# Two token groups in turn: the first 128 prompt tokens go through the trunk of a hybrid decoder step alone, and their expert rows are fetched while the other 136 tokens go through it

## The reference, cut to what matters

```python
def layer(x):                                  # x: 256 prompt rows, then 8 sample rows
    z, xbc, dt, q, k, v, iq, ik, iw, g_a, g_b = split(rms_norm(x, norm1_g) @ w_in)   # 1024 -> 10368
    y_ssd = ssd(conv(xbc), dt, z)              # prompt: 2 chunks of 128, state handed on; sample: one step
    y_att = sparse_attention(q, k, v, iq, ik, iw)   # prompt: best 64 keys; sample: best 256 of a paged cache
    merged = sigmoid(g_a) * (y_ssd @ w_branch_a) + sigmoid(g_b) * (y_att @ w_branch_b)
    x = x + merged @ w_out
    return x + peer(rms_norm(x, norm2_g))

def peer(h, p):
    q = (h @ p['peer_wq']).reshape(n, 8, 2, 128)
    s = einsum('nhcd,chkd->nhck', q, p['peer_keys'])        # 2 x 128 scores a head
    s1, i1 = top_k(s[:, :, 0], 16);  s2, i2 = top_k(s[:, :, 1], 16)
    top_s, pos = top_k(s1[..., :, None] + s2[..., None, :], 16)   # of 256 sums
    g = softmax(top_s)
    act = gelu(einsum('nd,nhkd->nhk', h, p['peer_u'][eidx]))
    return einsum('nhk,nhkd->nd', g * act, p['peer_v'][eidx])
```

## Time and profile before

| | before |
|---|---|
| median of 3 runs | 1549.29 us (1548.42 to 1551.8) |
| the profiled execution | 1551.73 us, its span 1550.1 us |
| mean granted TensorE clock | 0.944 |
| PE, DVE, ACT, POOL busy | 82%, 56%, 39%, 28% of the span |
| moved by the DMA engines | 391.08 MB, mean 252 GB/s |
| span up to the first expert gather | 859.65 us |

### The profile page before, as it was taken

One profiled execution on the slowest core, in us unless ns is written; L12 is line 12 of the kernel. 1 busy time (PEld: TensorE's weight loads), 2 busy tenths in 40 slices (PEclk: granted clock), 3 DMA queues, 4 the chain that ended last, 5 costly groups with the idle time before them and its releaser, 6 DMA issues. The chain is left out here.

```text
span 1550.1 us, 18152 instructions
## 1 busy us (share of the span) xinstructions
PE 1265.0 (82%) x4972; PEld 768.5 (50%) x4972; DVE 864.0 (56%) x2312; ACT 608.0 (39%) x1556; POOL 432.5 (28%) x510
## 2 busy tenths in 40 slices
PE   5968999999677877699989678977976787878777
PEld 4846678777555555488878323322322322222222
DVE  1025459998192427650110798898995554544544
ACT  1125237878382414500001345443533444444443
POOL 1331002220121200000000354644787333333331
PEclk8978999999697988999999799999999999999999
DMA  4543223322387630144142799999996999999997
GB/s 157 171 156 99 80 82 122 110 96 93 129 311 288 207 106 1 67 173 169 55 158 87 313 421 400 421 421 409 397 421 284 419 422 423 421 422 422 422 422 317
DMA packets 77066, 391.08 MB, mean 252 GB/s; under 512 B 11384, under 2 KB 22168, under 8 KB 39616
## 3 DMA queue, kind: packets, MB, share of 16 engines
q0 software_dynamic: 43168, 287.34, 45.4%
q1 hardware_dynamic: 33088, 101.32, 18.8%
q10 hardware_dynamic: 736, 1.56, 0.3%
HBM read 378.43 MB, written 11.60 MB: 252 GB/s over the span
## 5 line engine op out<-in xcount | busy, mean ns | idle before, releaser
L1706 PE MATMUL pe_acc<-pe_uv,pe_dg 128*128 128x512 f32 (+1 forms) x1056 | 524.8, 624 | 147.5 <-ACT pe_dg L1752 143.9
L1932 DVE CUSTOM_DVE_ANT_0 pe_uv<-pe_uv,pe_hnat 128x1024 f32<-128x1024 f32 x264 | 321.4, 1219 | 195.5 <-DMA pe_uv<-d_uv,pe_idx 183.9
L1706 PEld LDWEIGHTS pe_acc<-pe_uv,pe_dg 128*128 128x128 f32 (+1 forms) x1056 | 180.1, 189 | 488.8 <-ACT pe_dg L1752 342.3
L1799 POOL DMA_INDIRECT pe_uv<-d_uv,pe_idx x256 | 319.1, 1246 | 337.4 <-PE pe_acc L1706 314.1
L180 PE MATMUL pi_ps<-xn,pi_w 128*128 128x264 f32 x944 | 226.6, 397 | 9.5 <-PEq L86 9.5
L180 PEld LDWEIGHTS pi_ps<-xn,pi_w 128*128 128x128 f32 x944 | 182.4, 197 | 42.2 <-issue 11.3
L1746 ACT ACTIVATE pe_gl<-pe_a 128x1 f32<-128x1 f32 x264 | 53.4, 202 | 351.4 <-DVE pe_a L1932 348.6
L1752 ACT ACTIVATE pe_dg<-cst,pe_w 128x128 f32<-128x128 f32 x256 | 102.8, 401 | 8.3
L1749 ACT ACTIVATE pe_w<-pe_gl,pe_gw 128x1 f32<-128x1 f32 x256 | 75.4, 295 | 31.5
L1781 POOL COPY pe_hrep<-hN 128x128 f32<-128x128 f32 x8 | 1.9, 295 | 298.0 <-POOLq L86 298.0
L1613 PE MATMUL pq_ps<-hN,pq_w 128*128 128x264 f32 x256 | 58.7, 393 | 5.7 <-DMA pq_w<-d_wq 5.7
(11 more groups left out here) (283 smaller groups left out, 1707.8 us busy)
## 6 DMA issues: line engine op xcount, KB each, us to landing
pi_w<-d_w_in SPq DMA_DIRECT2D x71, 512.0 KB, 3.3
mg_w<-d_w_ab SPq DMA_DIRECT2D x8, 1536.0 KB, 6.7
ss_h<-d_state SPq DMA_DIRECT2D x8, 1024.0 KB, 7.1
o_ssm_s<-ss_h SPq DMA_DIRECT2D x8, 1024.0 KB, 7.1
pq_w<-d_wq SPq DMA_DIRECT2D x16, 512.0 KB, 3.3
lg_w<-d_w_in SPq DMA_DIRECT2D x10, 512.0 KB, 6.1
paged<-d_ck POOLq DMA_DIRECT2D x32, 128.0 KB, 5.5
paged<-d_ck SPq DMA_DIRECT2D x32, 128.0 KB, 5.5
```

The source lines that it names most:

```text
L1706: mm = pe.matmul(acc[0:m, 4 * half:4 * half + 4, :], lhsT, uv[:, r, D_MODEL + half * 512:D_MODEL + (half + 1) * 512], start=False, stop=Fa ...
L1799: pool.indirect_dma_start(uv[:, r, :], None, k.d_uv[:], bass.IndirectOffsetOnAxis(ap=src, axis=0)).then_inc(gathered[r], 16)
L1932: dve.tensor_tensor_reduce(uv[:, r, 0:D_MODEL], uv[:, r, 0:D_MODEL], hnat[:, n, :], 1.0, 0.0, ALU.mult, ALU.add, a[:, r:r + 1]).then_inc(d ...
```

## The change

Token group 0 is the first 128 prompt tokens, group 1 the other 128 prompt tokens and the 8 samples (136 columns). The 81 projection tiles are still computed once, for all 264 tokens, and their results are written to two sets of buffers. From there the blocks run twice, in this order: `attend_prompt(0)` (16 slots; all 32 rounds of the sample's top-256 and 44 tiles), `time_steps` (now 6 tiles), `ssd_chunk(0)`, `merge(0)`, `queries(0)`; then `attend_prompt(1)`, `attend_sample`, `ssd_chunk(1)`, `merge(1)`, `queries(1)`. `merge` and `queries` load all of their weights in both turns. `LastGates` is gone.

The experts are a class now. Units go in pairs; a pair is three pieces of code, which the blocks of group 1 put behind their own work of slot m on DVE, of slot m+1 on ACT and of slot m+2 on PE. Group 0's 64 pairs are dealt out over five blocks; the other 68 run at the end of `queries(1)`. The ring has 6 slots. A unit's product is four matmuls of 64 rows and 64 columns of the array in place of two of 128 by 128; for it ACT makes two 128x64 folded diagonals. In the diff `END` is all 81 tiles, `j` is `p % 8` (a head has 8 pairs), and `attend` runs all up to `merge(0)`. K and V pages come on SP's queue alone.

```diff
-    ends = [Z0, Z0 + 6, Z0 + 14, END - BANKS, END]
+    ends = [Z0, Z0 + 6, Z0 + 14, END - 6, END]
...
+    ends = [0, 12, 36, 43, 54, 64]
+    pairs = [list(range(a, b)) for a, b in zip(ends, ends[1:])]
...
+            attend(nc, k, prompt)
+            ex = Experts(nc, last, k)
+            queries(nc, k, ex, 0, [])
+            k.hankel[1], = tensors(nc, prompt, hankel1=(P, HEADS, TP))
+            attend_prompt(nc, k, 1, [], ex, pairs[0])
+        attend_sample(nc, k, ex, pairs[1])
+    k.Y[1], k.rms[1] = tensors(nc, trunk, Y1=(P, KI, W), rms1=(P, GROUPS, W))
+    ssd_chunk(nc, k, 1, ex, pairs[2])
+    merge(nc, k, 1, ex, pairs[3])
...
+            queries(nc, k, ex, 1, pairs[4])
...
+def late(at, m, lag):
+    return at[m - lag] if 0 <= m - lag < len(at) else []
...
+class Experts:
+    RING, PAIRS = 6, 4
+    def gathers(self, pool, pairs):
+        end = min(2 * pairs[-1] + 2 + self.RING, self.UNITS) if pairs else self.RING
+        for u in range(self.sent, end):
+            n, i = self.tile(u)
+            if n < 2 and i % TOPK == 0:
+                pool.wait_ge(self.indexed, self.choice(u) + 1)
+            if n == 2 and i == 0:
+                pool.wait_ge(self.moved, 64)
+            if u >= self.RING:
+                pool.wait_ge(self.accumulated, u - self.RING + 1)
+            pool.indirect_dma_start(self.uv[:, u % self.RING, :], None, self.k.d_uv[:], ...)
+        self.sent = end
+    def dots(self, dve, p):
+        for u in (2 * p, 2 * p + 1):
+            dve.wait_ge(self.gathered[r], 16 * (u // self.RING + 1))
+            dve.tensor_tensor_reduce(self.uv[:, r, 0:D_MODEL], self.uv[:, r, 0:D_MODEL], h[:], ...)
+        if j == 0:
+            self.choosing = self.choose(dve, follows)    # the next head's choice, in 21 pieces
+        if j < 4:
+            for _ in range(7):
+                next(self.choosing, None)
+        elif j == 6:
+            self.weights(dve, follows)
+    def weigh(self, act, p):
+        act.wait_ge(self.dotted, 2 * p + 2)
+        act.activation(self.gl[:, q, :], self.a[:, q, :], ACT.Gelu_apprx_tanh).then_inc(self.gelued, 1)
+...
+    def mix(self, pe, p):
+        for u in (2 * p, 2 * p + 1):
+            pe.wait_ge(self.diagonal, u + 1)
+            for half in range(2):
+                for q in range(2):
+                    rows = slice(q * HD, (q + 1) * HD)
+                    mm = pe.matmul(self.acc[half * HD:(half + 1) * HD, q, :], self.dg[rows, r, :],
+                                   self.uv[rows, r, vals], start=False, stop=False, ...)
+            mm.then_inc(self.accumulated, 1)
...
 def ssd_chunk, DVE's list, for g in range(GROUPS):
                 dve.wait_ge(em_ready, g + 1)
                 dve.tensor_tensor(mx[:, g % 2], em[:, g % 2], cb[:, g, :]..., ALU.mult).then_inc(mixed, 1)
+                for p in late(at, g, 0):
+                    ex.dots(dve, p)
...
 def merge, PE's list, for n in range(KD):
-                branch(n, pa, range(KI), lambda c: k.Y[:, c, :]).then_inc(multiplied, 1)
+                branch(n, pa, range(KI), lambda c: Y[:, c, :]).then_inc(multiplied, 1)
+                for p in late(at, n, 2):
+                    ex.mix(pe, p)
...
 def attend_sample, POOL's list:
-            for visit in range(2 * VK):
-                load(pool, by_pool, 1, visit)
+            ex.gathers(pool, todo)
```

More of the change, by code:

```diff
@@ L51 @@
 GATE0 = XBC0 + N_XBC
[L52 to L53 removed]
+END = N_TILES
 Q0, K0, V0, IQ0 = 0, 8, 10, 12
@@ L661, in _, with attend_prompt @@
             dve.wait_ge(read, 1)
-def attend_prompt(nc, k, tiles):
+def attend_prompt(nc, k, part, tiles, ex=None, pairs=()):
     NL, NPR, LAG_T, LAG_O = 3, 4, 2, 3
@@ L908, in _, with ssd_chunk @@
             mm.then_inc(widened, 1)
-def ssd_chunk(nc, k, c):
-    t0 = c * P
+            for n in tiles[3:]:
+                k.proj.multiply(pe, n)
+def ssd_chunk(nc, k, c, ex=None, pairs=()):
+    xbc, zs, Y, rms = k.xbc[c], k.zs[c], k.Y[c], k.rms[c]
+    W = PARTS[c][1] - PARTS[c][0]
+    at = shares(pairs, GROUPS)
     with ExitStack() as ctx:
@@ L1259, in load @@
                 eng.wait_ge(mixed, visit - VK - NG + 1)
-            for i in (2 * half, 2 * half + 1):
+            for i in range(GP):
                 if visit < VK:
@@ L1390, in _ @@
                     ssd.fade(act, n // 2)
-            for g in after[VK]:
-                gates.evacuate(act, g)
+                if n % 2 == 1:
+                    for p in late(when, n // 2, 1):
+                        ex.weigh(act, p)
             act.wait_ge(negated, 1)
@@ new lines, in _ @@
+        @block.gpsimd
+        def _(pool):
+            if last:
+                pool.memset(wide[:], 0.0).then_inc(cleared, 1)
+                for c in range(KD):
+                    pool.wait_ge(normed, c + 1)
+                    pool.tensor_copy(hrep[:, c, :].rearrange("p (r b) -> p r b", b=TS),
+                                     hN[:, c, P:W].unsqueeze(1).broadcast_to([P, P // TS, TS])).then_inc(repeated, 1)
+                ex.gathers(pool, rest)
+            else:
+                ex.gathers(pool, pairs)
@@ new lines, in _ @@
+            if not last:
+                for _ in ex.choose(dve, 0):
+                    pass
+                ex.weights(dve, 0)
+                return
+            start = None
+            for n in range(NT):
+                for p in late(at, n, 0):
+                    ex.dots(dve, p)
+                if n == 4:
+                    start = ex.choose(dve, first)
+                if 4 <= n < NT - 2:
+                    for _ in range(4):
+                        next(start, None)
+                if n == NT - 3:
+                    for _ in start:
+                        pass
+                if n == NT - 1:
+                    ex.weights(dve, first)
@@ L1978, in attend @@
             score_sample(nc, k)
-            attend_prompt(nc, k, part[2])
-        time_steps(nc, k, part[3])
-    attend_sample(nc, k)
+            attend_prompt(nc, k, 0, part[2])
+            time_steps(nc, k, part[3])
+        k.Y[0], k.rms[0] = tensors(nc, early, "right", Y0=(P, KI, P), rms0=(P, GROUPS, P))
+        ssd_chunk(nc, k, 0)
+        merge(nc, k, 0)
 def build(nc, ins, outs):
```

1032 lines of the change are left out of this document (539 added, 493 removed).

## The result

| | before | after |
|---|---|---|
| median | 1550.55 us (1548.42 to 1552.57, 4 runs) | 1568.52 us (1564.67 to 1571.38, 4 runs) |
| ratio to before | | 1.0115, 95% interval 1.0085 to 1.0144 |
| span of the profiled execution | 1550.1 us | 1569.8 us |
| first gather | 859.65 us | 560.40 us |
| mean granted TensorE clock | 0.944 | 0.842 |

The forecast was 1530 us, faster, with a range of 1465 to 1600. The time lies in the range and on the other side of before.

The account below looks back on a forecast made before the run. Gathers on DMA were taken to bound the experts, with DMA room in the trunk to hide them. 588 us for group 0 plus 942 for group 1 and the tail gave 1530 us, faster, range 1465 to 1600.

Parts of the forecast that it names:

- The bound: In the experts, gathers set the cost: 2.485 us a unit at 422 GB/s, 656 us for 264 units.
- group 0: From the start to the end of queries(0), the first group's blocks were summed to 588 us.
- merge(0): In group 0's merge, 528 passes of 0.124 us, a 9.3 us weight wait and a 6 us tail: 81 us.
- queries(0): In group 0's queries, 5.8 us at the start, 296 passes of 0.124 us and 3 at the end: 46 us.
- no cost with 3 us of slack: In the gather ring, six slots leave 8.8 us for landing against at least 5.6, so they cost nothing.
- rival C: In the blocks with hidden units, the ring of six starves if gathers land late: +70, 1600 us; chance 0.22.
- a median under 9 us: In the gather queue, such a median from issue to landing would rule out ring starvation; near 15 would confirm it.
- queries(1): In group 1's queries, 46 us plus 20 units at 0.9 us and 3 more: 67 us.
- the tail: After the slots of queries(1), 130 more units at 2.485 us, 323, plus start-up, reloads and end: 357 us.
- B: In group 1's blocks, hiding is nearly complete: DMA floor 1396, 1404 with the end, or 1467 us; chance 0.25.
- D: In the units' product on PE, tiles don't run side by side: 3.4 to 3.85 us a unit, 1715 us and more; chance 0.03.
- E: In the tail, the TensorE clock falls, a unit takes 1.8 us on PE at 1.2 GHz: +25, 1555 us; chance 0.08.

Follow-up runs that it names:

- e1: The changed kernel without POOL's drain at the ends of blocks from queries(0) on, semaphores kept to the end: 1544.21 us, ratio 0.9955 to the kernel before.
- e9: The changed kernel without drains, with seven ring slots and six of merge's eight output weight tiles in used-up branch-weight space: 1522.98 us, ratio 0.9824 to before.
- e4: The changed kernel with five slots in the ring in place of six: 1663.48 us, ratio 1.0707 to the kernel before.
- e11: e9 with six ring slots and the original buffers elsewhere, merge's output weights still in used-up branch-weight space: 1544.37 us, ratio 0.9953 to before.
- e2: The changed kernel with no pair inside a block, all 264 units at the end, group 0's choices all made in queries(0): 1735.26 us, ratio 1.1195 to before.
- e7: The changed kernel without drains, with the first weights of merge(1) loaded already in ssd_chunk(1): 1545.58 us, ratio 0.9954 to before.
- e10: e9 with two pairs in every second or third slot of attend_prompt(1), not one in three slots of four: 1560.24 us, ratio 1.0063 to before.
- e12: e9 with the 64 pairs dealt 16, 24, 8, 10, 6 in place of 12, 24, 7, 11, 10: 1533.51 us, ratio 0.9901 to before.
- e3: The changed kernel with a unit's value product as 128x128 matmuls again, and three output-weight slots in place of four: 1604.28 us, ratio 1.0349 to before.
- e6: The changed kernel without drains, with seven ring slots and smaller buffers for merge's output weights and the turned keys: 1542.93 us, ratio 0.9938 to before.

## Why the prediction was wrong

**The bound, and group 0.** Right. Experts cost what gathers cost, and the first group's blocks take 587.3 us against 588. Inside the sum `merge(0)` was 9 us too dear (3 of them because a 128-column pass is 62.39/529 = 0.118 us, not 0.124) and `queries(0)` 6 too cheap, so that the total is better than its parts. The first gather is at 560.4 and not at 588 because the choice of the first head is ready in the middle of that block. It can win little: six gathers fill the ring, and the first product that frees a slot comes with the next block (the seventh gather is issued at 612.25).

**The step that failed: what a block's end costs.** I took the blocks' ends from the kernel before, where PE stands idle 1 to 4 us, or 6 to 9 with a wait for first weights, and put the hiding units between them as if a boundary had nothing to do with them. In the kernel before only one long chain of gathers existed, in the last block, and its only boundary was the end. Its own drain of 18.66 us there was in the trace for the taking, at 1525.66, and one of 7.50 at 549.91, where pages on POOL's queue had been in flight. Both ended 5 to 6 us before their blocks' last work did, which is why the blocks' ends looked cheap. The edit puts four boundaries across gathers in flight. Four drains of 8.9 to 11.0 us followed, and without them the kernel is 24.3 us faster (e1): enough to turn +18 into -7 us against before. No rival of mine had this mechanism. It was a wait that the change adds, and every engine stands behind it.

**The second step: "no cost with 3 us of slack" for six slots.** I took a landing of at least 5.6 us from a gather issued into empty queues, and set it against 8.8. In a full ring of six landing is 8.9 us in the median, of seven 11.1 (e9) and of eight 15.1, and the loop of five and of six both last 15.3 us (e4): there is no slack of 3 us. Seven slots win 21 us (e11 against e9). So rival C was right in its mechanism and too high in its price (+70), since the medians of landing by block are 8 to 11.5 us and not 15. Its sign was no help: the prediction takes a median under 9 us as the end of C, and the median is 8.9, with 21 us lost all the same. In the two profiles, whose spans differ by 22.3 us, `queries(1)` and the tail are 12.8 us apart, `attend_sample` 6.0, `attend_prompt(1)` 4.2 and the rest 1 or less, with group 0 on the other side by 1.9.

**The sum otherwise.** Both terms removed (e9), the median is 1523 us against 1530. That is nearer than the parts are: in e9 the four blocks ahead of `queries(1)` are 21 us shorter than forecast, and `queries(1)` and the tail 10 longer. In e1 the block terms stood within 5 us, except `queries(1)`, 77.4 us against 67, and the tail, 364 against 357. The units in `queries(1)` cost 1.7 us each and not the 0.9 of the product alone: PE waits 7.9 us for diagonals, and DVE 32 for gathers ahead of them, and the first weights come 3 us later than in the block without units (e2). Two sums of the prediction are off by 4 us, and cancel: 68.6 − 3.7 + 79.5 is 144 and not 148 in `attend_sample`, and the terms given for `ssd_chunk(1)` make 84 and not 80.

**B, nearly complete hiding**, was far off: its floor of 1404 took 422 GB/s for everything and no order. e2 shows that two fifths of a hidden unit are hidden. e7, e10 and e12 point to two sides of why: in `merge(1)` DMA is nearly full, and in `attend_prompt(1)` the order in the lists binds, by far the more when units come in fours (e10).

**D** was wrong as held (e3, 0.94 us a unit). **E** came in part: the tail's granted clock is 0.82, with PE busy 128 of 240 us, where it was 1.00 with 192 of 240 (and 0.96 with 174 in e3), and most products of a pair there take either 1.95 us or 3.2 to 3.7. The Trainium skill, TensorE: Matmul & The Clock Gate, Part 1, has the clock follow PE's activity as well, and the trace agrees in direction (0.82, not 0.5). What it cost in time wasn't tried apart. The longer product stands in the part of the loop that is not landing, and six slots leave no room for it; that this makes it cost time was not shown.

**What stays open.** How the 21 us of the seventh slot divide between tail and blocks is read from one profile of each kernel, not tried. Why the sample attention takes 18 us more without a unit was not tried either, nor what the lower clock costs.

## What to carry to other kernels

Work that is in flight across a block boundary meets whatever that boundary waits for: look in the trace for what ends a block on each engine, queue by queue, before you lay transfers over it. Size a ring of buffers by the landing time in a full ring, and not by a single transfer's, and remember that it grows with the slots (8.9, 11.1 and 15.1 us for six, seven and eight here). And count a hidden unit as partly hidden: here it cost 1.2 to 1.9 us in its block against 2.55 at the end.

## What the runs showed of the hardware

- A DRAIN on POOL at a block's end lasts until the indirect DMAs that POOL issued have landed: 8.87 to 10.97 us at four places and 12.17 and 26.70 at two more, with up to six gathers of 1 MB in flight, and 18.66 in the kernel before, with up to eight. It ends 0.3 to 2.2 us after the last landing each time.
- The DMA engines' busy share reads 1.00 to 1.01 with 407 to 411 (e1 and the changed kernel), 419 (e6) and 422 GB/s (before) for rings of six, seven and eight gathers of 1 MB, and 0.93 with 343 for five (e4). With six and a longer product (e3) it reads 1.00 with 395.
- Sixteen 64-row, 64-column passes of 512 columns on four tiles take 1.87 us from start to start between 128x128 matmuls, both changes of shape included.
